# Starting bytes of weight buffers and operands moved by 64 in a two-block transformer kernel

## The chip, the core and the metric

The kernel runs as one launch on one core of a Trainium2 chip. The metric is the device time of that launch in microseconds (us), the median of the runs. Matrix products run on TensorE (PE); its weight loads are listed apart (PEld), since they run beside its matmuls. VectorE (DVE), ScalarE (ACT) and GpSimd (POOL) do the rest, and SyncE (SP) issues the weight transfers.

## What is computed

Two blocks, one after the other, on 256 tokens of width 1024. The first block also carries 256 context tokens. In its first layer all 512 tokens need an output; in its last layer (`l = 1`) the context is only read, so most products there move 256 tokens. The second block moves 256 tokens throughout.

```python
def first_block(...):            # DEPTH = 2
    for l in range(DEPTH):
        x, xc = trunk_layer(...)     # rmsnorm, w_in, latent attention + pooling + gated linear
                                     # attention, merge of the three branches, w_out, rmsnorm
def second_block(...):           # DEPTH = 2
    for layer in range(DEPTH):
        h = rmsnorm_2(x, norm_mix_pre[layer])
        m = attention_mixer(h, ...) if layer % 2 == 0 else recurrent_mixer(h, ...)
        x = x + rmsnorm_2(m, norm_mix_post[layer])
        h = rmsnorm_2(x, norm_ffn_pre[layer])
        x = x + rmsnorm_2(swiglu(h, ...), norm_ffn_post[layer])
def swiglu(h, w_gate, w_up, w_down):             # hidden width 2816
    return (jax.nn.silu(h @ w_gate) * (h @ w_up)) @ w_down
```

## The kernel before

**The weight stream.** All large weights come as 384 "halves" of 128 x 1024 fp32 words (`STREAM`, indexed by k). SP sends half k to a slot of SBUF (`RAW`), ACT rounds it to its high part (`WH`, line 1280), DVE forms the low part (`WL`, line 1874, in the place of the raw words), and TensorE multiplies. A slot is 8 KB in each partition: `WL` in the first 4 KB, `WH` in the last 4. `slots()` gives each half the least recently used slot of those that `free_slots(k)` allows; the order of the halves is fixed.

**One column.** A product of fp32 accuracy is three passes: high weights by high activations, high by low, low by high. `column(k, ...)` (its matmuls are recorded at line 651, in the helper `product`) does this over eight 128-row tiles, so one half is 24 matmuls, each with 128 columns of weights held and 256 tokens moved past them. I call such a group of 24 a column. `some_columns` (line 669) does three columns at once, tile by tile, behind a norm; `pre_normed` (lines 1054 and 1056) does the fourth, with one plain fp32 product of ones by `PB_` in its middle. The down projection has its matmuls at line 1083, its last three halves at line 1094, and `last_column` (line 730) ends the other projections. In `token_rows` (line 1066) the activations are held and the weights move.

**Places.** SBUF places are written by hand as byte offsets from `base`, which lies on a multiple of 128. Slots 0 to 3 stand at 0, 8, 16 and 24 KB. Everything after the held constants stands at `kb(n)`, which is `o + n * 1024`; the sizes of the held tensors make `o` 56384, that is 64 modulo 128. So slots 0 to 3 start at 0 modulo 128, and every other slot and every moving operand (`XH`, `XL`, `XH2`, `XL2`, `YH`, `YL`, `HH`, `HL`, `AH`, `AL`, `CH`, `CL`) at 64 modulo 128. Steps inside a slot or an operand are multiples of 128 bytes. Where 256 tokens move, a column whose weights stand in slots 0 to 3 thus **differs** modulo 128 from what moves past it; a column in any other slot is **alike** to it.

**Which slot when.** From the second block on the slots go round in a cycle of nine: 10, 11, 12, 8, 2, 9, 3, 0, 1, so five columns of nine are alike. The 40 columns of line 651 in the first feed-forward are 21 alike and 19 different, in the second 23 and 17; the 19 columns of line 1083 are 12 and 7 in the first, 10 and 9 in the second. From `merge, 1` to `rg_out` other slots (17, 27 to 33) take part as well. In the order of TensorE's rows below, the number behind the underscore is only the number of the allocation.

Of the kernel before, what the change touches and what calls it, by code (L numbers as in the profile page):

```python
# [9 lines left out]
KT = D // P  # L10
SEQ, CTX = 256, 256
# [14 lines left out]


HALF = 8 * P
PLAN = {}


def plan():
    at = 0
    for l in range(DEPTH):
        for name, n in (("mod", 12), ("win", 12), ("gv", 2), ("merge", 18), ("wout", 4)):
            PLAN[name, l] = at
            at += n
    for name, n in (("attn_qk", 8), ("attn_v", 4), ("attn_out", 4), ("gate_up0", 22), ("down0", 11),
                    ("rg_in", 8), ("rg_ai", 2), ("rg_out", 4), ("gate_up1", 22), ("down1", 11)):
        PLAN[name] = at  # L40
        at += n
# [63 lines left out]
def mod_halves(p):  # L105
# [3 lines left out]
    at = [4 * quarter + rows_ for quarter in ((s, s + 2) if p < MOD_START else (2 * s, 2 * s + 1))]  # L109
    return [2 * PLAN["mod", 0] + a if a < 24 else 2 * PLAN["mod", 1] + a - 24 for a in at]  # L110

# [18 lines left out]
def stream():  # L130
# [13 lines left out]
    for l in range(DEPTH):  # L144
        win = PLAN["win", l]
        for b in FIRST:
# [3 lines left out]
        for place in steps_of(l):  # L150
            for kind, i in place:
# [4 lines left out]
                elif kind == "gv":  # L156
                    group(("gv", l, i), PLAN["gv", l], 2 * i, 2)
                else:
                    mod_pair(i)
        group(("merge", l), PLAN["merge", l], 0, 36)  # L160
        group(("wout", l), PLAN["wout", l], 0, 8)
# [23 lines left out]
STREAM, AT = stream()  # L185
# [29 lines left out]
LATE = BLOCK2 + 5  # L215

HIDDEN, DOWN_LATE = 5, AT["down0"] + 9
NSLOT = 34
END, MORE = 28, 5


def free_slots(k):

    if k < MOD_START:
        return [0, 1, 2, 3, 5, 13, 14, 15, 16]
    if k < AT["z", 0, FIRST[0]]:
        return [0, 1, 2, 3, 5, 14, 16]
    if k < AT["g", 0, 0]:
        return [4, 6, 7, 17]
    if k in WHOLE and k < AT["merge", 0]:  # L230
        return [25, 26]
    if k < AT["merge", 0] + END:
        return [0, 1, 2, 3]
    if k < AT["wout", 0] + 8:
        return [0, 1, 2, 3, 7, 17]
    if k < AT["z", 1, FIRST[0]]:
        return [18, 19, 20, 21, 22, 23, 24, 25]
    if k < AT["g", 1, 0]:
        return [0, 1, 2, 3, 7, 8, 17]
    if k < AT["merge", 1] + MORE:  # L240
        return [0, 1, 2, 3, 8]
    if k < AT["merge", 1] + END + 3:
        return [0, 1, 2, 3, 8, 27, 28]
    if k < BLOCK2:
        return [0, 1, 2, 3, 8, 10, 17, 27, 28]
    more = [29, 30, 31] if AT["rg_x"] <= k < AT["rg_a0"] else [32, 33] if DOWN_LATE <= k < AT["rg_x"] else []
    return [0, 1, 2, 3, 8, 9, 10] + ([11, 12] if k >= LATE else []) + more

OPENED = ((7, AT["merge", 0] + END, AT["merge", 0] + 25), (17, AT["merge", 0] + END, AT["merge", 0] + 25),
          (25, AT["g", 0, 0], AT["g", 0, 0]), (26, AT["g", 0, 0], AT["g", 0, 0]),
          *((s, AT["wout", 0] + 8, AT["wout", 0] + 1) for s in range(18, 26)), (8, AT["z", 1, FIRST[0]], AT["wout", 0] + 3),
          (27, AT["merge", 1] + MORE, AT["merge", 1] + 1), (28, AT["merge", 1] + MORE, AT["merge", 1] + 1),
          (10, AT["merge", 1] + END + 3, AT["merge", 1] + 25), (17, AT["merge", 1] + END + 3, AT["merge", 1] + 25),
          (29, AT["rg_x"], AT["down0"] + HIDDEN), (30, AT["rg_x"], AT["down0"] + HIDDEN), (31, AT["rg_x"], AT["attn_out"] + 8),
          (32, DOWN_LATE, AT["down0"]), (33, DOWN_LATE, AT["down0"]),
          (9, BLOCK2, AT["wout", 1] + 3), (11, LATE, AT["wout", 1] + 8), (12, LATE, AT["wout", 1] + 8))


def slots():

    slot, nth, before, last, uses = [], [], [], {}, {}
    for k in range(HALVES):
        s = min(free_slots(k), key=lambda s: last.get(s, -1))
        uses[s] = uses.get(s, 0) + 1
        slot.append(s)
        nth.append(uses[s])
        before.append(max([last.get(s, -1) + 1] + [count for s_, first, count in OPENED if s_ == s and k >= first]))
        last[s] = k  # L270
    return slot, nth, before

# [30 lines left out]
def program(nc, x_t, wstream, small, vecs, consts, rel, consts2, out_t):  # L303
    f32 = mybir.dt.float32
    f32r = mybir.dt.float32r
# [4 lines left out]
    LN_EXP, EXP_TANH = "natural_log_exp_and_others", "exp_and_others"  # L310

    with ExitStack() as ctx:
        base = (nc.sbuf_base + 63) // 64 * 64
        KB_ = 1024

        def sb(name, at, *shape, dt=f32):
            return nc.alloc_sbuf_tensor_at(name, [P, *shape], dt, offset=base + int(at))
# [6 lines left out]
        at = 48 * KB_  # L324
# [8 lines left out]
        MOD, AMOD, GPOST = held("MOD", DEPTH * 3 * KT, 2), held("AMOD", DEPTH * KT, 2), held("GPOST", DEPTH * KT, 2)  # L333
        NLAM, PLAM, LT = held("NLAM", KT), held("PLAM", KT), held("LT", 2, KT)
        STAT, SELT, R2C = held("STAT", 2, 8), held("SELT", 4), held("R2C", 2)
        o = at

        def kb(n):
            return o + n * KB_

        SLOT_AT = [8 * KB_ * i for i in range(4)] + [kb(113), kb(121), kb(133), kb(141), kb(48), kb(134), kb(142), kb(16), kb(24),
                                                   kb(0), kb(8), kb(16), kb(24), kb(80),
                                                   *(kb(103 + 4 * i) for i in range(7)), kb(134), kb(138),
                                                   kb(109), kb(125), kb(62), kb(70), kb(126), kb(0), kb(8)]
        RAW = [sb(f"RAW{i}", a, HALF) for i, a in enumerate(SLOT_AT)]
        WL = [sb(f"WL{i}", a, HALF, dt=f32r) for i, a in enumerate(SLOT_AT)]
        WH = [sb(f"WH{i}", a + 4 * KB_, HALF, dt=f32r) for i, a in enumerate(SLOT_AT)]

# [10 lines left out]
        WIDE = [TOK, SEQ]  # L361
        ZG = [sb(f"ZG{l}", kb(32), 12, w) for l, w in enumerate(WIDE)]
        YL = [sb(f"YL{l}", kb(32), 12, w, dt=f32r) for l, w in enumerate(WIDE)]
        YH = [sb(f"YH{l}", kb(133), 4, w, dt=f32r) for l, w in enumerate(WIDE)]
        Z = sb("Z", kb(56), 12, TOK)
        VG = sb("VG", kb(80), 4, 512)
        SW = sb("SW", kb(88), SW_MORE + NSW)
# [4 lines left out]
        CS = sb("CS", kb(150), SEQ + 2 * PADW)  # L372
        DF = sb("DF", kb(151) + 64, SEQ)
        MG = [sb(f"MG{l}", kb(101), KT, w) for l, w in enumerate(WIDE)]
        SG = [sb(f"SG{l}", kb(117), KT, w) for l, w in enumerate(WIDE)]
        EX, EM = sb("EX", kb(88), 4, TOK), sb("EM", kb(96), TOK)
        E1 = sb("E1", kb(56), TOK)
        QE, KDT = sb("QE", kb(68), TOK), sb("KDT", kb(70), NCH, P)
# [3 lines left out]
        LG = Z[:, Z_POOL:Z_POOL + 4, :]  # L382


        M = sb("M", kb(32), KT, SEQ)
        SQ2 = sb("SQ2", kb(40), KT, SEQ)
        PA = sb("PA", kb(56), 2, SEQ)
        PB_ = sb("PB", kb(58), SEQ)
        R1, R2, R2Q = sb("R1", kb(59), SEQ), sb("R2", kb(60), SEQ), sb("R2Q", kb(61), SEQ)
        aS, aA = kb(62), kb(78)  # L390
        XH2 = sb("XH2", kb(0), KT, SEQ, dt=f32r)
        XL2 = sb("XL2", kb(8), KT, SEQ, dt=f32r)

# [71 lines left out]

        raw_in = [sem(f"raw_in{i}") for i in range(NSLOT)]
        hi_ready, lo_ready, halves_done = sem("hi_ready"), sem("lo_ready"), sem("halves_done")
# [94 lines left out]
        def _(pool):  # L562
# [17 lines left out]
            def post_sum(blocks):  # L580
                sum_blocks(msq_ready, SQ2, PA, PB_, blocks, lambda b: b)
                n.next(msq_ready, KT)
# [48 lines left out]
        def _(pe):  # L631
# [102 lines left out]
            def first_block(l):  # L734
                t, w = query_tokens(l), WIDE[l]
                ring = (0, 1) if l == 0 else (0, 1, 2)
                zg, yh, yl = ZG[l], YH[l], YL[l]

# [286 lines left out]
                for kt in some_columns(k0, outs3, xh, xl, range(KT)):  # L1025
                    pe.wait_ge(xl_ready, n.next(xl_ready))
                pb, sq = (PB0, SQ) if l == 0 else (PB_, SQ2)
                for i in range(3, 7):
# [40 lines left out]
            def ffn(i):  # L1069
# [18 lines left out]
                for m in range(KT):  # L1088
                    if m == KT - 1:
                        sums = take(4)  # L1090
                        post_sum_part(sums, SEQ, PB_, SQ2, 4)
                    for u in range(FB - TAIL, FB):
# [4 lines left out]
                    if m < KT - 1:  # L1097
                        last.then_inc(down_ready, 1)
                post_sum_end(sums, SEQ, SQ2)

            def attention():
# [109 lines left out]
                for i in range(3, 7):  # L1211
                    column(k0 + i, take((0, 1, 2, 6, 7)[i % 5])[:, 0:SEQ], lambda kt: AH[:, kt, :], lambda kt: AL[:, kt, :])
                last_column(k0 + 7, take(2)[:, 0:SEQ], lambda kt: AH[:, kt, :], lambda kt: AL[:, kt, :], SEQ, PB_, SQ2)

# [45 lines left out]
        def _(act):  # L1260
# [57 lines left out]
            def first_block(l):  # L1318
                t, w = query_tokens(l), WIDE[l]
                zg, yh, sg, mg = ZG[l], YH[l], SG[l], MG[l]  # L1320
                lead = (4 if l == 0 else 5) - 2
# [217 lines left out]
            def normed_block(m, b, gain):  # L1539

                A(SQ2[:, m, :], BANK[b][:, 0:SEQ], ACT.Square).then_inc(msq_ready, 1)
                A(M[:, m, :], BANK[b][:, 0:SEQ], ACT.Copy, scale=gain(m)).then_inc(bank_free[b], 1)

# [310 lines left out]
        def _(dve):  # L1854
# [93 lines left out]
            def first_block(l):  # L1948
                t, w = query_tokens(l), WIDE[l]
                zg, yh, yl, sg, mg = ZG[l], YH[l], YL[l], SG[l], MG[l]  # L1950
                lead = (4 if l == 0 else 5) - 2
# [346 lines left out]
            def boundary(gain):  # L2298
# [5 lines left out]
                def scaled(c):  # L2304
                    k0, k1 = CHUNKS[c]
                    v.tensor_tensor(M[:, k0:k1, :], M[:, k0:k1, :], R1[:, :].unsqueeze(1).to_broadcast([P, k1 - k0, SEQ]),
                                    ALU.mult).then_inc(mr_step, 1)
                    n.next(mr_step)

                def added(c):  # L2310
                    k0, k1 = CHUNKS[c]
                    dve.wait_ge(mr_step, m0 + c + 1)
                    v.tensor_tensor(X[:, k0:k1, XT], X[:, k0:k1, XT], M[:, k0:k1, :], ALU.add).then_inc(x_new, 1)

# [406 lines left out]
```

## Time and profile before

| what | value |
|---|---|
| median of 3 runs | 1565.04 us (1564.38 to 1567.49) |
| the profiled execution: device time | 1563.12 us |
| its span, first to last instruction | 1561.3 us |
| TensorE busy, matmuls | 1457.5 us, 93% |
| VectorE, ScalarE busy | 897.9 us (58%), 723.2 us (46%) |
| chain of work that ended last: TensorE's share | 81% |
| mean granted TensorE clock | 0.972 |

A matmul of 256 columns is recorded with a duration of about 280 ns, but matmuls overlap in the array: what a stretch costs is the distance from the start of one to the start of the next. A start is given to 0.01 us, so the distance is best read over the 24 matmuls of a column. The mean durations by group of instructions don't tell it.

### The profile page before, as it was taken

What the parts mean: (1) busy time and instruction counts of PE and PEld (TensorE: products, weight loads), DVE (VectorE), ACT (ScalarE), POOL (GpSimd) and SP (SyncE); (2) the same over time, 40 slices, a digit from 0 to 9 for tenths busy, and PEclk for the clock granted to TensorE, in tenths of its full rate; (3) what the DMA queues carried; (4) which work ended last, traced back from release to release, by engine and by line L of the source; (5) the groups of instructions that cost most, each with busy time, mean ns of one, the idle gap of its engine ahead of it and who ended that gap; (6) DMA issues with size and microseconds to landing.
All of it is one profiled execution on the core that took longest, in us unless ns stands there. A gap on an engine that the chain in (4) does not pass through costs nothing.

```text
span 1561.3 us, 23755 instructions
## 1 busy us (share of the span) xinstructions
PE 1457.5 (93%) x9888; PEld 1263.1 (81%) x9888; DVE 897.9 (58%) x1495; ACT 723.2 (46%) x1164; POOL 98.8 (6%) x125
## 2 busy tenths in 40 slices
PE   4999999999999998999999899989999988899997
PEld 2676766787877776777988799878999988899997
DVE  4455663535443625776376558766666567766642
ACT  4433333523325244544545545665444468644442
POOL 0200000000000030000000010001221000112200
PEclk8999999899999999999999999999999999899998
DMA  8433333122223271232344455424656625356661
GB/s 341 128 108 123 121 122 115 50 80 80 82 71 113 73 259 43 93 95 68 107 150 135 150 189 195 135 92 152 189 189 210 229 76 176 109 182 189 186 189 52
DMA packets 58841, 212.56 MB, mean 136 GB/s; under 512 B 6448, under 2 KB 7728, under 8 KB 58736
## 3 DMA queue, kind: packets, MB, share of 16 engines
q1 hardware_dynamic: 57408, 205.29, 40.3%
q0 software_dynamic: 1328, 5.77, 1.2%
q8 instruction: 79, 1.29, 0.3%
q14 instruction: 26, 0.21, 0.0%
HBM read 209.98 MB, written 1.05 MB: 135 GB/s over the span
## 4 chain that ended last, share of the span: by engine, by line
PE 81%; DVE 10%; ACT 5%; DMA 1%; issue 1%; SPq 0%; POOL 0%; ACTq 0%; DVEq 0%; POOLq 0%
PE B L651 51%; PE B L669 8%; PE B L1083 7%; DVE WL L1874 3%; PE B L795 3%; ACT WH L1280 2%; PE B L1066 1%; DMA RAW<-wstream 1%; PE B L1094 1%; PE B L681 1%; PE B L875 1%; PE B L862 1%; PE B L989 1%; PE B L730 1%; PE B L1056 1%
## 5 line engine op out<-in xcount | busy, mean ns | idle before, releaser
L1874 DVE TENSOR_TENSOR WL<-RAW,WH 128x1024 fp32r<-128x1024 f32 x336 | 412.4, 1235 | 384.5 <-ACT WH L1280 383.0
L651 PE MATMUL B<-XH,WH 128*128 128x256 f32 (+1 forms) x1600 | 510.9, 319 | 4.3 <-DVE ZG L2085 2.7
L651 PE MATMUL B<-XL,WH 128*128 128x256 f32 (+1 forms) x1600 | 495.2, 309 | 0.0
L651 PE MATMUL B<-XH,WL 128*128 128x256 f32 (+1 forms) x1600 | 495.1, 309 | 0.0
L1280 ACT ACTIVATE WH<-RAW 128x1024 fp32r<-128x1024 f32 x336 | 346.4, 1052 | 112.3 <-DMA RAW<-wstream 112.0
L651 PEld LDWEIGHTS B<-XH,WH 128*128 128x128 f32 x1600 | 305.1, 191 | 31.7 <-issue 7.9
L651 PEld LDWEIGHTS B<-XL,WH 128*128 128x128 f32 x1600 | 305.2, 191 | 21.3 <-issue 5.9
L651 PEld LDWEIGHTS B<-XH,WL 128*128 128x128 f32 x1600 | 305.0, 191 | 17.0
L669 PE MATMUL B<-XH,WH 128*128 128x256 f32 (+1 forms) x208 | 73.4, 353 | 25.3 <-DVE XL L2318 13.3
L1083 PE MATMUL B<-HH,WL 128*128 128x256 f32 x304 | 85.3, 280 | 0.0
L1083 PE MATMUL B<-HH,WH 128*128 128x256 f32 x304 | 85.2, 280 | 0.0
L1083 PE MATMUL B<-HL,WH 128*128 128x256 f32 x304 | 85.2, 280 | 0.0
L1586 ACT ACTIVATE SIL<-T 128x256 f32<-128x256 f32 x44 | 18.4, 418 | 121.0 <-DVE T L2335 121.0
L651 PE MATMUL B<-YH,WH 128*128 128x512 f32 (+1 forms) x192 | 66.0, 344 | 8.3 <-DVE ST L2202 6.6
L669 PEld LDWEIGHTS B<-XH,WH 128*128 128x128 f32 x208 | 44.4, 214 | 34.5 <-issue 24.4
L669 PE MATMUL B<-XL,WH 128*128 128x256 f32 (+1 forms) x208 | 71.8, 345 | 0.0
L669 PE MATMUL B<-XH,WL 128*128 128x256 f32 (+1 forms) x208 | 71.5, 344 | 0.0
L1387 ACT ACTIVATE PR<-B,STAT 128x512 f32<-128x512 f32 (+1 forms) x48 | 29.6, 616 | 87.6 <-DVE STAT L2075 87.6
L1502 ACT ACTIVATE SG<-B 128x512 f32<-128x512 f32 (+1 forms) x48 | 23.5, 490 | 97.1 <-PE B L651 97.1
L651 PE MATMUL B<-YL,WH 128*128 128x512 f32 (+1 forms) x192 | 64.7, 337 | 0.0
L651 PE MATMUL B<-YH,WL 128*128 128x512 f32 (+1 forms) x192 | 64.6, 337 | 0.0
L575 POOL TENSOR_TENSOR PA<-SQ 128x512 f32<-128x512 f32 (+1 forms) x6 | 11.6, 1938 | 805.4 <-ACT SQ L1521 482.9
(326 smaller groups left out, 2444.6 us busy)
## 6 DMA issues: line engine op xcount, KB each, us to landing
RAW<-wstream SPq DMA_DIRECT2D x384, 512.0 KB, 3.5
X<-x_t SPq DMA_DIRECT2D x4, 512.0 KB, 6.6
SW<-small POOLq DMA_DIRECT2D x2, 896.0 KB, 8.5
SW<-small POOLq DMA_DIRECT2D x2, 768.0 KB, 7.3
BT<-rel POOLq DMA_DIRECT2D x1, 1024.0 KB, 15.1
X<-consts POOLq DMA_DIRECT2D x1, 768.0 KB, 8.6
out_t<-X SPq DMA_DIRECT2D x3, 256.0 KB, 2.4
BT<-rel POOLq DMA_DIRECT2D x1, 512.0 KB, 10.8
```

Of the source, the lines that this page charges most:

```text
L651: last = mm(out, w, x, start=i == 0, stop=i == len(pairs) - 1)
L669: last = mm(out, w[:, kt * P:(kt + 1) * P], x(kt, h), start=i == 0 and p == 0, stop=i == KT - 1 and p == 2)
L681: last = mm(bank[at:at + 32, :], cv[:, 2 * (p % 4) + j, :], raw_of(k + c)[:, j * 512:(j + 1) * 512], start=p % 4 == 0, stop=p % 4 == 3, ti ...
L730: last = mm(out, wt[:, kt * P:(kt + 1) * P], x(kt), start=kt == 0 and p == 0, stop=kt == KT - 1 and p == 2)
L795: last = mm(bank, x[:, kt, rows_], wt[:, cols], start=kt == 0 and p == 0 and tb % 2 == 0, stop=kt == KT - 1 and p == 2, skip_group_check=True)
L862: last = nc.tensor.transpose(bank[:, k * P:(k + 1) * P], PR[:, u % 2, k * P:(k + 1) * P], ident)
L1083: last = mm(outs[m][:, 0:SEQ], w[:, m * P:(m + 1) * P], h[:, u, :], start=u == 0 and p == 0, stop=False)
L1280: A(hi_of(h), raw_of(h), ACT.Copy).then_inc(hi_ready, 1)
L1387: A(PR[:, u % 2, 0:nk], BANK[b][:, 0:nk], ACT.Exp, bias=STAT[:, u % 2, 0:1], accum_out=STAT[:, u % 2, 1:2]).then_inc(bank_free[b], 1)
L1502: A(sg[:, i, :], bank_of("G", l, b, i)[:, 0:w], ACT.Tanh, scale=0.5).then_inc(free("G", l, b, i), 1)
L1586: A(SIL[:, f % 2, :], T1[:, f % 2, :], ACT.Silu).then_inc(silu_ready, 1)
L1874: v.tensor_tensor(lo_of(h), raw_of(h), hi_of(h).bitcast(f32), ALU.subtract).then_inc(lo_ready, 1)
```

## The change

`base` is rounded to 128 instead of 64 (it comes to the same byte), and `o` is written so that it is 64 modulo 128 (it comes to the same byte as well). The slots used where 256 tokens move are shifted by 64 bytes (9, 10 and 31 by 192) and so start at 0 modulo 128: 9 to 12 and 27 to 33. Slot 8, which also serves the last layer of the first block, keeps its place; from `wout, 1` on a new slot 34, the same place plus 64 bytes, takes its turns, and `OVER` makes it wait for slot 8's last reader. Slots 0 to 7 and 13 to 26 keep their places; of these slot 17 has a turn in `merge, 1` and in `wout, 1`. Around the shifted slots the tensors of the second block make room: `M`, `SQ2`, `PA`, `PB_`, `R1`, `R2`, `R2Q` and everything at `aS` move by 64 bytes, everything at `aA` (`HH`, `HL`, `AH`, `AL`, `CH`, `CL` among them) by 128, `YH` and `SG` of layer 1 by 128 and 64.

No instruction is added or removed, and the order is the same on every engine; which half waits for which (`BEFORE`) is the same too. Only the slot's name changes, as here on TensorE in the first feed-forward, at the step from one column to the next. Before:

```order
L651 MATMUL B6<-XH2_216,WH12_141 128x256
L651 MATMUL B6<-XL2_217,WH12_141 128x256
L651 MATMUL B6<-XH2_216,WL12_107 128x256
L651 MATMUL B7<-XH2_216,WH8_137 128x256
L651 MATMUL B7<-XL2_217,WH8_137 128x256
L651 MATMUL B7<-XH2_216,WL8_103 128x256
```

After:

```order
L665 MATMUL B6<-XH2_219,WH12_143 128x256
L665 MATMUL B6<-XL2_220,WH12_143 128x256
L665 MATMUL B6<-XH2_219,WL12_108 128x256
L665 MATMUL B7<-XH2_219,WH34_165 128x256
L665 MATMUL B7<-XL2_220,WH34_165 128x256
L665 MATMUL B7<-XH2_219,WL34_130 128x256
```

Slot 34 stands where slot 8 stood; nothing else has moved in the row of instructions.

```diff
@@ free_slots(k)
+    if k < AT["wout", 1]:
+        return [0, 1, 2, 3, 8, 10, 17, 27, 28]
     if k < BLOCK2:
-        return [0, 1, 2, 3, 8, 10, 17, 27, 28]
+        return [0, 1, 2, 3, 34, 10, 17, 27, 28]
     more = [29, 30, 31] if AT["rg_x"] <= k < AT["rg_a0"] else [32, 33] if DOWN_LATE <= k < AT["rg_x"] else []
-    return [0, 1, 2, 3, 8, 9, 10] + ([11, 12] if k >= LATE else []) + more
+    return [0, 1, 2, 3, 34, 9, 10] + ([11, 12] if k >= LATE else []) + more
@@ slots()
+OVER = {34: (8,)}
+    def read(s):
+        return max(last.get(other, -1) for other in (s, *OVER.get(s, ())))
@@ program(...)
-        base = (nc.sbuf_base + 63) // 64 * 64
+        base = (nc.sbuf_base + 2 * LINE - 1) // (2 * LINE) * 2 * LINE
-        o = at
+        o = at + (LINE - at) % (2 * LINE)
-        SLOT_AT = [8 * KB_ * i for i in range(4)] + [kb(113), kb(121), kb(133), kb(141), kb(48), kb(134), kb(142), kb(16), kb(24),
-                                                   kb(0), kb(8), kb(16), kb(24), kb(80),
+        SLOT_AT = [8 * KB_ * i for i in range(4)] + [kb(113), kb(121), kb(133), kb(141), kb(48), kb(134) + 3 * LINE, kb(142) + 3 * LINE,
+                                                   kb(16) + LINE, kb(24) + LINE, kb(0), kb(8), kb(16), kb(24), kb(80),
                                                    *(kb(103 + 4 * i) for i in range(7)), kb(134), kb(138),
-                                                   kb(109), kb(125), kb(62), kb(70), kb(126), kb(0), kb(8)]
+                                                   kb(109) + LINE, kb(125) + LINE, kb(62) + LINE, kb(70) + LINE, kb(126) + 3 * LINE,
+                                                   kb(0) + LINE, kb(8) + LINE, kb(48) + LINE]
-        YH = [sb(f"YH{l}", kb(133), 4, w, dt=f32r) for l, w in enumerate(WIDE)]
+        YH = [sb(f"YH{l}", kb(133) + 2 * LINE * l, 4, w, dt=f32r) for l, w in enumerate(WIDE)]
-        PB_ = sb("PB", kb(58), SEQ)
+        PB_ = sb("PB", kb(58) + LINE, SEQ)
-        aS, aA = kb(62), kb(78)
+        aS, aA = kb(62) + LINE, kb(78) + 2 * LINE
```

`LINE` is 64.

## Rows read from the trace of the kernel before

**Rows 1.** The page: chain that ended last, shares by engine.

```profile
PE 81%; DVE 10%; ACT 5%; DMA 1%; issue 1%; SPq 0%; POOL 0%; ACTq 0%; DVEq 0%; POOLq 0%
```

**Rows 2.** Chain in order of time (start, us, what), both feed-forwards.

```profile
1081.36 112.15 PE B L651 x960
1193.51 53.60 PE B L1083 x456
...
1374.78 112.48 PE B L651 x960
1487.26 53.28 PE B L1083 x456
```

**Rows 3.** Timeline of PE (start, duration): columns in slots 1, then 10.

```profile
1114.78 0.28 PE L651 MATMUL B<-XH,WH 128*128 128x256 f32 x1
...
1117.50 0.28 PE L651 MATMUL B<-XH,WH 128*128 128x256 f32 x1
...
1120.38 0.28 PE L651 MATMUL B<-XH,WH 128*128 128x256 f32 x1
```

**Rows 4.** The same view, line 1066, weights moving: end of slot 9, slot 3.

```profile
968.00 0.28 PE L1066 MATMUL B<-WH,XL 128*128 128x256 f32 x1
...
969.08 0.28 PE L1066 MATMUL B<-WH,XL 128*128 128x256 f32 x1
...
970.13 0.28 PE L1066 MATMUL B<-WH,XL 128*128 128x256 f32 x1
...
972.17 0.28 PE L1066 MATMUL B<-WH,XL 128*128 128x256 f32 x1
```

**Rows 5.** The same view: a column in slot 1 behind a plain fp32 product.

```profile
950.15 0.59 PE L1054 MATMUL B<-PB,C 128*128 128x256 f32 x2
950.40 0.47 PE L1056 MATMUL B<-XH,WH 128*128 128x256 f32 x1
950.70 0.28 PE L1056 MATMUL B<-XL,WH 128*128 128x256 f32 x1
...
951.88 0.28 PE L1056 MATMUL B<-XH,WL 128*128 128x256 f32 x1
```

**Rows 6.** The same view, recurrent mixer, slot 3, then 0 and 1.

```profile
1292.21 0.38 PE L651 MATMUL B<-CH,WH 128*128 128x256 f32 x1 [0.87 <-DVE XR L2335]
...
1297.26 0.28 PE L651 MATMUL B<-XH,WH 128*128 128x256 f32 x1
...
1300.09 0.28 PE L651 MATMUL B<-XH,WH 128*128 128x256 f32 x1
```

**Rows 7.** Windows: busy us (instructions) of each engine, PEclk, DMA share, GB/s.

```profile
1080.00:1190.00 110.00, 110.00 (x943) 110.00 (x942) 71.33 (x105) 50.81 (x66) 22.72 (x40) 1.00 0.62 195
1193.00:1246.00 53.00, 53.00 (x453) 53.00 (x452) 30.92 (x27) 27.18 (x26) 2.00 (x2) 1.00 0.70 236
1274.00:1371.00 97.00, 86.01 (x668) 84.04 (x667) 75.92 (x115) 70.06 (x117) 5.87 (x3) 0.93 0.43 136
```

**Rows 8.** Chain in order of time: the second block's attention, then the recurrent mixer.

```profile
952.16 11.51 PE B L651 x96
...
996.51 3.03 PE B L651 x24
...
1047.91 11.04 PE B L651 x96
...
1319.72 1.24 DVE IG L2530
...
1330.20 11.57 PE B L669 x79
```

More of the change, by code:

```diff
@@ L28 @@
 HALF = 8 * P
+LINE = 64
 PLAN = {}
@@ L217 @@
 HIDDEN, DOWN_LATE = 5, AT["down0"] + 9
-NSLOT = 34
+NSLOT = 35
 END, MORE = 28, 5
@@ L255 @@
           (10, AT["merge", 1] + END + 3, AT["merge", 1] + 25), (17, AT["merge", 1] + END + 3, AT["merge", 1] + 25),
-          (29, AT["rg_x"], AT["down0"] + HIDDEN), (30, AT["rg_x"], AT["down0"] + HIDDEN), (31, AT["rg_x"], AT["attn_out"] + 8),
+          (34, AT["wout", 1], AT["merge", 1] + 25), (29, AT["rg_x"], AT["down0"] + HIDDEN), (30, AT["rg_x"], AT["down0"] + HIDDEN), (31, AT["rg_x"], AT["attn_out"] + 8),
           (32, DOWN_LATE, AT["down0"]), (33, DOWN_LATE, AT["down0"]),
           (9, BLOCK2, AT["wout", 1] + 3), (11, LATE, AT["wout", 1] + 8), (12, LATE, AT["wout", 1] + 8))
+OVER = {34: (8,)}
 def slots():
     slot, nth, before, last, uses = [], [], [], {}, {}
+    def read(s):
+        return max(last.get(other, -1) for other in (s, *OVER.get(s, ())))
     for k in range(HALVES):
-        s = min(free_slots(k), key=lambda s: last.get(s, -1))
+        s = min(free_slots(k), key=read)
         uses[s] = uses.get(s, 0) + 1
@@ L268, in slots @@
         nth.append(uses[s])
-        before.append(max([last.get(s, -1) + 1] + [count for s_, first, count in OPENED if s_ == s and k >= first]))
+        before.append(max([read(s) + 1] + [count for s_, first, count in OPENED if s_ == s and k >= first]))
         last[s] = k
@@ L374, in program @@
         MG = [sb(f"MG{l}", kb(101), KT, w) for l, w in enumerate(WIDE)]
-        SG = [sb(f"SG{l}", kb(117), KT, w) for l, w in enumerate(WIDE)]
+        SG = [sb(f"SG{l}", kb(117) + LINE * l, KT, w) for l, w in enumerate(WIDE)]
         EX, EM = sb("EX", kb(88), 4, TOK), sb("EM", kb(96), TOK)
@@ L382, in program @@
         LG = Z[:, Z_POOL:Z_POOL + 4, :]
-        M = sb("M", kb(32), KT, SEQ)
-        SQ2 = sb("SQ2", kb(40), KT, SEQ)
-        PA = sb("PA", kb(56), 2, SEQ)
-        PB_ = sb("PB", kb(58), SEQ)
-        R1, R2, R2Q = sb("R1", kb(59), SEQ), sb("R2", kb(60), SEQ), sb("R2Q", kb(61), SEQ)
-        aS, aA = kb(62), kb(78)
+        M = sb("M", kb(32) + LINE, KT, SEQ)
+        SQ2 = sb("SQ2", kb(40) + LINE, KT, SEQ)
+        PA = sb("PA", kb(56) + LINE, 2, SEQ)
+        PB_ = sb("PB", kb(58) + LINE, SEQ)
+        R1, R2, R2Q = sb("R1", kb(59) + LINE, SEQ), sb("R2", kb(60) + LINE, SEQ), sb("R2Q", kb(61) + LINE, SEQ)
+        aS, aA = kb(62) + LINE, kb(78) + 2 * LINE
         XH2 = sb("XH2", kb(0), KT, SEQ, dt=f32r)
```

## The prediction

> **What bounds the kernel now.** I read the chain of work that ended last first: TensorE has 81% of it [rows 1]. The second block shows where: each feed-forward is one unbroken piece, 960 matmuls at line 651 and 456 at line 1083 [rows 2], and the windows over both kinds show TensorE busy all the time, VectorE 71.33 of 110 us at most, the DMA engines at 0.62 to 0.70, the clock at 1.00, which is its 2.4 GHz level [rows 7]. So there the time is matmuls times their distance, and the distance is what to look at next. The timeline gives it over a column of 24. In slot 1, which differs modulo 128 from what moves, a column takes 1117.50 - 1114.78 = 2.72 us, 113.3 ns a matmul. The next, in slot 10, alike, takes 1120.38 - 1117.50 = 2.88 us, 120.0 ns [rows 3]. The instructions, the lengths and the clock are the same.
>
> Does this hold for all? It can be tested on whole pieces. First feed-forward, line 651: 21 alike and 19 different columns, 21 x 2.88 + 19 x 2.72 = 112.16 us; the chain has 112.15. Second: 23 and 17, 112.48; the chain has 112.48. Line 1083: 12 and 7, 53.60; 10 and 9, 53.28; both are as in the chain [rows 2]. So two numbers explain the four pieces. Where the roles are swapped (line 1066, weights move, activations are held) the same pair shows: nine matmuls in 969.08 - 968.00 = 1.08 us, 120.0 ns, in slot 9, and eighteen in 972.17 - 970.13 = 2.04 us, 113.3 ns, in slot 3 [rows 4]. The sign of the difference doesn't matter, then, which bears on the slots moved by 192 and on the operands moved by 128.
>
> **A third distance.** It is the weak point of the change. After a break in TensorE's row, different columns often settle at another distance. Behind the fp32 product by `PB_`, ten matmuls in slot 1 take 951.88 - 950.70 = 1.18 us, 118 ns [rows 5]; after the wait at 1292.21 a whole column in slot 0 or 1 takes 1300.09 - 1297.26 = 2.83 us, 117.9 ns [rows 6]. I call this the slow pace. Of the different columns that I followed behind a break about two thirds take it and a third goes to 113.3. It passes over the step from one different column to the next. In the second block I see it end only in a column that is alike: the next different one is at 113.3 again. The change takes away all alike columns there, and with them what ends the slow pace.
>
> **The change part by part.** (1) *Columns that become different.* Feed-forwards: 24 + 14 + 25 + 11 = 74. At 113.3 each saves 0.16 us: 74 x 0.16 = 11.8 us, all on the chain. Rest of the second block: 35. Behind the norm of the attention 4 x 24 matmuls run unbroken, 11.51 us = 119.9 ns each [rows 8]: the 6 columns of the first projections give 1.0 us. The 7 of the second projections stand singly between softmax steps, and five begin with a break. Here I take the slow pace: a different column with its break is 3.03 us [rows 8], 2.83 and a restart of 0.2, so 0.05 each, with 0.16 for the two of line 1066: 0.6 us. The output projection's 4: 0.5 us. The recurrent mixer's 18 would give 2.9 us, but TensorE is busy only 86.01 of 97 us there [rows 7], the wait in rows 6 is for VectorE's `XR`, and the chain passes through VectorE's `IG` [rows 8]: half, 1.4 us. Last layer of the first block: 13 columns (slots 27, 28, 10, and 34 for 8), between breaks, at 0.05: 0.7 us. Sum: 11.8 + 1.0 + 0.6 + 0.5 + 1.4 + 0.7 = 16.0 us.
>
> (2) *Columns that lose the reset.* Each feed-forward enters behind the `PB_` product, where the slow pace begins (rows 5; I saw it the same way in the other column of this kind whose slot differs). A column at the slow pace instead of 113.3 gives up 0.11 us. The bounds are: none stays slow, 0; all 118 columns of lines 651 and 1083 stay slow, 118 x 2.83 = 333.9 us against 331.5 now [rows 2], so +2.4 us instead of -11.8. The trace doesn't show which: the longest unbroken slow stretch of different columns is some 60 matmuls [rows 6], the longest at 113.3 eight columns at most, but with hundreds of such matmuls and no fall to the slow pace without a break. Whatever ends the slow pace need happen only once in each feed-forward. `PB_` itself moves, too, so that its last pass is now alike to the weight load behind it, which may set either pace. I take the slow pace for about ten columns in all: +1 us.
>
> (3) *Supply.* At 2.72 us a column, VectorE's 71.33 us and ScalarE's 50.81 us for 40 columns [rows 7] stand against 108.8 us of TensorE: they hide. The transfers go from 0.62 to about 0.64 of the DMA engines. Nothing is late next in the feed-forwards. If the cover were gone, TensorE would wait for `WL`, at VectorE's rate, still under 2 us a column. The order and the counts of the slots' waits are unchanged, so slot 34 costs nothing.
>
> (4) *Moved places of the other operands.* No length of VectorE or ScalarE work in the trace depends on the slot's place, so 0; bounds: -1 to +1 us.
>
> The sum is -16.0 + 1 = -15 us. The profiled execution has 1563.12 us (a span of 1561.3 us and 1.8 around it), 1.9 under the median of the runs, so 1565.0 - 15 = 1550 us.
>
> The Trainium skill, page "TensorE: Matmul & The Clock Gate", section "Step-by-step: what each phase is for", speaks against this: TensorE has two independent SBUF read ports, and loading the next weights takes nothing from the running matmul. By that rule places would not matter, and the time would stay 1565. Rows 3 and 4 disagree with the rule, by 6.7 ns a matmul; the rival below on the region carries what is left of it.
>
> **The rivals.**
>
> *Lock: the slow pace holds.* It enters behind `PB_` and nothing ends it. Feed-forwards +2.4 us; elsewhere the alike columns gain 48 x 0.05 = 2.4 us, and some 24 different ones that are at 113.3 now lose 0.11 each, 2.6. Sum about +2.5: 1567. For it: both columns like rows 5, and the steps that the pace survived. Against it: it was never seen for longer than three columns.
>
> *Half: one feed-forward locked, or some ten to fifty columns slow in each.* -4 to -10 us: 1555 to 1561.
>
> *Region, not the remainder.* Slots 0 to 3 are also the only ones in the lowest 32 KB, so the pair in rows 3 could come from where they lie, not from the address modulo 128; the trace can't separate the two. Then a shift by 64 bytes changes nothing: 1565.
>
> *Slower: the lock, at a longer distance.* The places are new (differences of 64 the other way, `PB_` at 0 modulo 128), so the pace that the lock holds need not be 117.9 ns. The 118 columns take 331.5 us now, 117.1 ns on average; from (331.5 + 3.1) / 2832 = 118.2 ns on the kernel is slower than the measurement's bound, and at 120 ns it is 339.8 us, +8.3. Between them I take 118.8: +4.9, 1570. For it: some matmuls in transition take 119 and more. Against it: all settled different columns are at 113.3 or below 118.
>
> **How the numbers follow.** About 0.2%, 3.1 us, is what a measurement of this kernel can tell from no change. Chances: forecast 0.46, half 0.14, lock 0.24, region 0.06, slower 0.10. So faster 0.60; same 0.30, lock and region; slower 0.10. The forecast's own range is 1546 (all 122 columns at 0.16 us: -19.5) to 1554. The range for 8 in 10 leaves out the slower rival and the ends: 1546 to 1568.
>
> **What would show it.** Right: the second feed-forward's two pieces at 40 x 2.72 = 108.8 and 19 x 2.72 = 51.7 us, every column in slots 9 to 12 and 34 at 2.72 us. The lock: both pieces made of 2.83 us, 113.2 and 53.8, in slots 0 to 3 as well, where it is 2.72 now. Region: 2.88 and 2.72 side by side as in rows 3. The sum is wrong if TensorE begins to wait in the feed-forwards, or if the recurrent mixer keeps its length.

## The result, and the profile after

| | before | after |
|---|---|---|
| median, same series of runs | 1564.71 us (1563.98 to 1567.49) | 1553.92 us (1550.68 to 1554.48) |
| ratio, 95% interval | | 0.9931 (0.9911 to 0.9952) |
| profiled execution: device time, span | 1563.12, 1561.3 us | 1554.48, 1552.7 us |

The kernel is faster by 10.8 us. A second series of the changed kernel (`a0_again` below) gave 1552.14 against 1564.15, ratio 0.9929 (0.9911 to 0.9947), 12.0 us. 1550 was forecast.

The page's first lines and its shares of the chain, for [rows 1]: nothing but TensorE's time changed.

```profile
PE 1448.6 (93%) x9888; PEld 1251.4 (81%) x9888; DVE 897.2 (58%) x1495; ACT 723.7 (47%) x1164; POOL 98.9 (6%) x125
...
PE 81%; DVE 10%; ACT 5%; DMA 1%; issue 1%; SPq 0%; POOL 0%; ACTq 0%; DVEq 0%; POOLq 0%
```

The chain in order of time (start, us, what) for [rows 2]. The change adds 14 lines, so L651, L669, L1083 and L1094 of before are L665, L683, L1097 and L1108 here.

```profile
1081.76 109.35 PE B L665 x960
1191.11 52.11 PE B L1097 x456
...
1370.81 108.80 PE B L665 x960
1479.61 52.43 PE B L1097 x456
```

Both feed-forwards are still one unbroken piece, and the second one's first part is 108.80 us: 40 columns at 2.72 us and not one at another distance. The other three are a little above 108.8 and 51.7. The timeline of TensorE (start, duration) shows the reason, for [rows 3]. These are the first matmuls of five columns in a row, in slots 1, 10, 11, 12 and 34:

```profile
1090.08 0.28 PE L665 MATMUL B<-XH,WH 128*128 128x256 f32 x1
...
1092.90 0.28 PE L665 MATMUL B<-XH,WH 128*128 128x256 f32 x1
...
1095.73 0.28 PE L665 MATMUL B<-XH,WH 128*128 128x256 f32 x1
...
1098.46 0.28 PE L665 MATMUL B<-XH,WH 128*128 128x256 f32 x1
...
1101.18 0.28 PE L665 MATMUL B<-XH,WH 128*128 128x256 f32 x1
```

The columns in slots 1 and 10 take 2.82 and 2.83 us, those in slots 11 and 12 take 2.73 and 2.72. So the slow pace, there from the column behind the norm as rows 5 had it, passes over five columns of this line and ends in slot 11, with no alike column near. In the four pieces 5, 4, 0 and 7 columns are slow, 16 in all.

The windows (columns as in [rows 7]) for the first feed-forward's two parts and the recurrent mixer:

```profile
1080.00:1190.00 110.00, 110.00 (x966) 109.97 (x965) 71.82 (x106) 51.96 (x68) 23.99 (x42) 1.00 0.63 201
1192.00:1243.00 51.00, 51.00 (x449) 51.00 (x448) 30.19 (x26) 26.00 (x25) 2.00 (x2) 1.00 0.71 244
1270.00:1367.00 97.00, 85.41 (x666) 83.39 (x665) 75.83 (x114) 70.06 (x117) 5.86 (x3) 0.91 0.41 136
```

**Where the time went.** The chain rows of before and after divide the span at the same instructions:

| stretch | before | after | difference | forecast |
|---|---|---|---|---|
| up to the first feed-forward's piece | 1081.36 | 1081.76 | +0.4 | -3.3 |
| its two parts | 165.75 | 161.46 | -4.3 | -5.3 |
| from there to the second one's piece | 127.67 | 127.59 | -0.1 | -2.0 |
| its two parts | 165.76 | 161.23 | -4.5 | -5.3 |
| the rest | 20.76 | 20.66 | -0.1 | -0.2 |
| span | 1561.3 | 1552.7 | -8.6 | -16.0, and +1 for slow columns |

The first line hides something that isn't the change's. In the first layer, whose slots and order are untouched, after has 3.3 us more. TensorE alone over the same instructions (columns: TensorE busy, PEclk, DMA share, GB/s), first before, then after:

```profile
437.00:500.00 63.00, 59.15 (x275) 1.00 0.28 92
```

```profile
437.00:503.30 66.30, 62.45 (x273) 0.95 0.27 87
```

The granted clock was 1.00, the 2.4 GHz level, before, and 0.95 on average after; it fell to its 1.2 GHz level for two stretches of 3.4 us, and 0.05 x 66.3 = 3.3 us. Without that the first line would be -2.9, and the whole -12.0 us. These two are estimates for one place, not measurements: over the whole execution the granted clock was 0.972 before and after, so what the changed kernel lost here it was spared elsewhere. In the recurrent mixer it was 0.93 before ([rows 7]) and 0.91 after. The gain is therefore best read from the pieces at a clock of 1.00, which have -4.3 and -4.5 us.

### The profile page after: what moved, and what is told of

Its sections match the earlier page's. It is cut to its first block, busy times and chain, and to the rows that moved or that the text cites. A ratio compares the mean times of both kernels' runs of the same rounds, so it can differ in the third digit from the quotient of the medians.

```text
span 1552.7 us, 23755 instructions
## 1 busy us (share of the span) xinstructions
PE 1448.6 (93%) x9888; PEld 1251.4 (81%) x9888; DVE 897.2 (58%) x1495; ACT 723.7 (47%) x1164; POOL 98.9 (6%) x125
## 4 chain that ended last, share of the span: by engine, by line
PE 81%; DVE 10%; ACT 5%; DMA 1%; issue 1%; SPq 0%; POOL 0%; ACTq 0%; DVEq 0%; POOLq 0%
PE B L665 51%; PE B L683 8%; PE B L1097 7%; DVE WL L1888 3%; PE B L809 3%; ACT WH L1294 2%; PE B L1080 1%; DMA RAW<-wstream 1%; PE B L1108 1%; PE B L695 1%; PE B L889 1%; PE B L876 1%; PE B L1003 1%; PE B L744 1%; PE B L1070 1%
## 5 line engine op out<-in xcount | busy, mean ns | idle before, releaser
L665 PE MATMUL B<-XH,WH 128*128 128x256 f32 (+1 forms) x1600 | 507.6, 317 | 4.3 <-DVE ZG L2099 2.7
L665 PE MATMUL B<-XL,WH 128*128 128x256 f32 (+1 forms) x1600 | 491.5, 307 | 0.0
L665 PE MATMUL B<-XH,WL 128*128 128x256 f32 (+1 forms) x1600 | 491.4, 307 | 0.0
L1294 ACT ACTIVATE WH<-RAW 128x1024 fp32r<-128x1024 f32 x336 | 346.7, 1053 | 108.8 <-DMA RAW<-wstream 108.5
L665 PEld LDWEIGHTS B<-XH,WH 128*128 128x128 f32 x1600 | 303.0, 189 | 32.2 <-issue 8.2
L665 PEld LDWEIGHTS B<-XL,WH 128*128 128x128 f32 x1600 | 303.1, 189 | 21.7 <-issue 6.1
L665 PEld LDWEIGHTS B<-XH,WL 128*128 128x128 f32 x1600 | 302.9, 189 | 17.0
L683 PE MATMUL B<-XH,WH 128*128 128x256 f32 (+1 forms) x208 | 73.1, 352 | 25.3 <-DVE XL L2332 13.3
L1097 PE MATMUL B<-HH,WH 128*128 128x256 f32 x304 | 84.3, 277 | 0.0
L1097 PE MATMUL B<-HH,WL 128*128 128x256 f32 x304 | 84.3, 277 | 0.0
L1097 PE MATMUL B<-HL,WH 128*128 128x256 f32 x304 | 84.2, 277 | 0.0
L665 PE MATMUL B<-YH,WH 128*128 128x512 f32 (+1 forms) x192 | 66.8, 348 | 8.3 <-DVE ST L2216 6.4
L683 PEld LDWEIGHTS B<-XH,WH 128*128 128x128 f32 x208 | 44.0, 212 | 34.7 <-issue 24.4
L683 PE MATMUL B<-XL,WH 128*128 128x256 f32 (+1 forms) x208 | 71.3, 343 | 0.0
L683 PE MATMUL B<-XH,WL 128*128 128x256 f32 (+1 forms) x208 | 71.1, 342 | 0.0
L665 PE MATMUL B<-YL,WH 128*128 128x512 f32 (+1 forms) x192 | 65.4, 340 | 0.0
L665 PE MATMUL B<-YH,WL 128*128 128x512 f32 (+1 forms) x192 | 65.1, 339 | 0.0
## 6 DMA issues: line engine op xcount, KB each, us to landing
BT<-rel POOLq DMA_DIRECT2D x1, 512.0 KB, 10.6
```

Of the source, the lines that this page charges most:

```text
L665: last = mm(out, w, x, start=i == 0, stop=i == len(pairs) - 1)
L683: last = mm(out, w[:, kt * P:(kt + 1) * P], x(kt, h), start=i == 0 and p == 0, stop=i == KT - 1 and p == 2)
L1097: last = mm(outs[m][:, 0:SEQ], w[:, m * P:(m + 1) * P], h[:, u, :], start=u == 0 and p == 0, stop=False)
L1294: A(hi_of(h), raw_of(h), ACT.Copy).then_inc(hi_ready, 1)
```

## The experiments

Each edit is against the changed kernel. Places are told from `base`, modulo 256. In the changed kernel slots 0 to 3, 9, 10 and 31 stand at 0, slots 11, 12, 27 to 30, 32, 33 and 34 at 128; `XH2` and `XL2` stand at 64, `HH`, `HL`, `AH`, `AL`, `CH` and `CL` at 192. I call a column **minus** when its weights stand 64 below what moves, and **plus** when 64 above. With `XH2` slots 0 to 3, 9 and 10 are minus and the others plus; with `HH` it is the reverse. In `token_rows`, where the weights move, I take the sign of what is held against what moves.

The theory: the difference of the two places modulo 128 decides. The rivals: the region of SBUF; a period of 256; any difference will do. Then, since 16 columns stayed slow: what sets the slow pace, and what ends it.

**Shift by 128 instead of 64** (`e1_by128`, one execution).

```diff
-        ... kb(134) + 3 * LINE, kb(142) + 3 * LINE, kb(16) + LINE, kb(24) + LINE, ...
+        ... kb(134) + 256, kb(142) + 256, kb(16) + 128, kb(24) + 128, ...
-        aS, aA = kb(62) + LINE, kb(78) + 2 * LINE
+        aS, aA = kb(62) + 128, kb(78) + 128
```

The other places that the change shifts by 64 are shifted by 128 too.

> The shifted slots are moved by 128 bytes (9, 10 and 31 by 256) instead of 64, so that they are alike to what moves modulo 128 again, but differ modulo 256; everything else is laid out as in the changed kernel. Theory (the remainder modulo 128 decides): columns in slots 9 to 12 and 34 take 2.88 us again, the feed-forward pieces about 112.2, 53.6, 112.5 and 53.3 us, total about 1564. Rival (a longer period, 256 or more, or any difference of places helps): 2.72 us, total about 1554.

```profile
1085.31 112.15 PE B L665 x960
1197.46 54.20 PE B L1097 x456
```

1568.80 us; one execution of before beside this and the next three runs had 1566.30. The first part is back at 112.15, to the last digit what [rows 2] has. A period of 256 falls: those columns are nowhere near 113.3 ns. That the sum is the same is chance, though: per matmul slots 9 and 10 take 120 ns with `XH2`, slots 11, 12 and 34, whose places are 128 off, mostly 118.5 to 118.9, and slot 2 behind them 117.7, where it had 113.3 before. Slots 3, 0 and 1 are at 113.3 with `XH2` but for their first turn in the second feed-forward, and with `HH` slots 0 to 3 are at 118 but for three columns. So 256 does play a part, in which distance beside 113.3 a column gets.

**The lowest slots made alike** (`e2_low_alike`, one execution). Slots 0 to 3, `X` and the held constants move up by 64; what stands behind them keeps its remainder.

```diff
-        SLOT_AT = [8 * KB_ * i for i in range(4)] + ...
+        SLOT_AT = [64 + 8 * KB_ * i for i in range(4)] + ...
```

> The changed kernel with slots 0 to 3 moved by 64 bytes, so that these four are now the ones alike to what moves, while slots 9 to 12 and 34 stay different. Theory (remainder): columns in slots 0 to 3 take 2.88 us wherever 256 tokens move, the others 2.72 or 2.83; the 40 columns of line 665 in the first feed-forward about 19 x 2.88 + 21 x 2.72 = 111.8 us. Where 512 tokens move, the columns in slots 0 to 3 come to 227 ns a matmul from about 231, some 5 us in all. Total about 1560. Rival (the lowest 32 KB of SBUF are a region of their own): slots 0 to 3 stay at 2.72 us, total 1554.

```profile
1084.23 111.84 PE B L665 x960
...
1374.92 111.74 PE B L665 x960
```

1562.19 us. The first is the 111.8 us expected. The roles have changed over: with `XH2` 120 ns in slots 0 to 3, 113.3 in slots 9 to 12 and 34, but for two columns at 117.8 at the start of the second. The region falls; it is the remainder.

**Shift by 32, and by 96** (`e3_by32`, `e4_by96`, one execution each).

```diff
-        ... kb(16) + LINE, kb(24) + LINE, ...
+        ... kb(16) + 32, kb(24) + 32, ...
```

> The shifted slots are moved by 32 bytes (9, 10 and 31 by 160) instead of 64: weights start 32 above what moves, modulo 128. Theory (two streams collide when they are in the same 64 bytes of a 128-byte line): 32 is half a collision, so a distance between 113.3 and 120.0 ns in slots 9 to 12 and 34, total 1556 to 1562. Rival A (any difference will do): 113.3 ns, total about 1554. Rival B (only exactly 64 helps): 120.0 ns, total about 1564.

> The shifted slots are moved by 96 bytes (9, 10 and 31 by 224): weights start 96 above, that is 32 below what moves, modulo 128. Theory (same 64 bytes): as with 32, a distance between 113.3 and 120.0 ns, total 1556 to 1562. Rival A (what counts is which stream is ahead): the two signs of 32 give different distances, one of them 113.3. Rival B (only exactly 64): 120.0 ns, total about 1564.

By 32, then by 96:

```profile
1078.54 113.65 PE B L665 x960
...
1372.41 111.92 PE B L665 x960
```

```profile
1081.96 113.31 PE B L665 x960
```

1561.04 and 1564.17 us. In the pieces shown first the moved slots take 118 to 120 ns with 32 and 117 to 119 with 96, and slots 0 to 3, whose own difference is still 64, are at 118 as well. So "any difference" falls too: among those tried only 64 gives 113.3 for a whole feed-forward. Nor are these 64's slow pace, brought in from the neighbours. In the second piece with 32, slots 0 to 3 are at 113.3 to 113.8 and the moved slots between them still at 118.2 to 119.7; at line 1097 with 96, slots 0 to 3 are at 113.3 to 114.2, slots 11, 12 and 34 at 116.7 to 116.8 and slots 9 and 10 mostly at 120.1. So 32 and 96 have distances of their own, mostly nearer to 120.0 than to 113.3.

**The changed kernel again** (`a0_again`, 6 executions).

> The changed kernel once more, beside the kernels that follow. Every theory: about 1554 us, ratio 0.993. Theory on the slow pace (it ends at a step from weights 64 below to weights 64 above what moves, modulo 256, and at no other step between different columns): the same columns as in its first profile are slow, those in slots 9, 3, 0, 1, 10 behind the product by PB_ in the first feed-forward, and if line 1097 starts slow, up to the step from slot 34 to slot 2. Rival (it ends by chance): other columns.

1552.14 us (1550.83 to 1556.51). The slow columns of its first feed-forward are the same nine, 109.35 and 52.11 us; in the second there are eight at line 665, where the first profile had none, and the same seven at line 1097. In the feed-forwards of both executions every slow stretch at line 665 ends from slot 10 to slot 11, every one at line 1097 from slot 34 to slot 2. With `XH2` and with `HH`, both are steps from a minus column to a plus one. That gave the next theory: the sign matters, and that step is what ends the slow pace.

**All columns plus** (`e5_plus`, 12 executions, and `e5_again`, 8).

```diff
-        SLOT_AT = [8 * KB_ * i for i in range(4)] + [..., kb(134) + 3 * LINE, kb(142) + 3 * LINE,
+        SLOT_AT = [128 + 8 * KB_ * i for i in range(4)] + [..., kb(134) + 320, kb(142) + 320,
-        aS, aA = kb(62) + LINE, kb(78) + 2 * LINE
+        aS, aA = kb(62) + 64, kb(78) + 256
```

> All slots used where 256 tokens move stand 64 bytes above what moves, modulo 256 (slots 0 to 3 and all behind them moved by 128, slots 9, 10 and 31 by 320 instead of 192, the operands of the second block and YH by 256). Slots 8 and 17 stay alike in the last layer of the first block. Theory (sign modulo 256): behind a break the slow pace ends within some five matmuls, no feed-forward column stays slow, pieces of lines 665 and 1097 at 108.8, 51.7, 108.8 and 51.7 us, total 1 to 4 us under the changed kernel, 1550 to 1553. Rival (chance): some columns stay slow as now, total 1554.

> The kernel of e5_plus once more, for a trace of one of its long executions: its profiled one took 1552.65 us, while most others took 1568 to 1571. Theory (with one sign the pace drawn behind the break holds): in an execution of 1568 us or more both feed-forwards are slow from end to end, pieces 113.1 and 53.7 us, as in e6_minus, 17 us over the fast one with the other second-block columns; an execution between, near 1560, has one feed-forward slow. Rival (something else is longer, such as waits for weights): pieces at 108.8 and 51.7 us, and the time is lost elsewhere.

The profiled execution of the first series had 1552.65 us:

```profile
1083.22 108.80 PE B L665 x960
1192.02 51.68 PE B L1097 x456
1369.76 108.80 PE B L665 x960
1478.56 51.68 PE B L1097 x456
```

That of the second had 1562.80 us:

```profile
1087.00 108.80 PE B L665 x960
1195.80 51.68 PE B L1097 x456
1373.35 113.07 PE B L665 x960
1486.41 53.71 PE B L1097 x456
```

All 118 columns fast in one; in the other 59 fast, then 59 slow from the first to the last (113.07 / 960 = 117.8 ns). The medians are 1568.84 us, ratio 1.0009 (0.9986 to 1.0032), and 1562.78, ratio 0.9987 (0.9953 to 1.0021): the gain is gone on average, yet single executions of this one kernel go from 1552.65 to 1571.0. The 20 of them lie in three groups: 2 at 1552.7 to 1552.8, 8 at 1559.2 to 1563.9, 10 at 1568.3 to 1571.0. That fits none, one and both feed-forwards slow, and the profiled ones are of the first and second group; one of the third wasn't profiled. Two feed-forwards alone would part the groups by 4.27 + 2.03 = 6.3 us each. Of the 10.2 us between the two profiled executions another 3.8 lie ahead of the first feed-forward, most of it between 860 and 895 us, where the granted clock was 1.00 in one and 0.91 in the other. My expectation, that the slow pace ends within a few matmuls behind a break, falls: it held for 1416 matmuls.

**All columns minus** (`e6_minus`, 12 executions).

```diff
-        ... kb(134) + 3 * LINE, kb(142) + 3 * LINE, kb(16) + LINE, kb(24) + LINE, ...
+        ... kb(134) + 448, kb(142) + 448, kb(16) + 192, kb(24) + 192, ...
```

> All those slots stand 64 bytes below what moves, modulo 256 (the shifts of 64 made 192, slots 9, 10 and 31 by 448, operands and YH by 256). Theory (sign modulo 256): the slow pace that begins behind the product by PB_ never ends inside a feed-forward: up to 40 x 2.83 = 113.1 us at line 665 and 19 x 2.83 = 53.7 at line 1097, both times, so that the gain is gone: 1560 to 1567. Rival (chance): about as the changed kernel, 1553 to 1556.

```profile
1082.23 113.07 PE B L665 x960
1195.30 53.71 PE B L1097 x456
1375.85 113.07 PE B L665 x960
1488.91 53.71 PE B L1097 x456
```

1565.27 us, ratio 1.0000 (0.9985 to 1.0016). Both feed-forwards are slow from end to end, in columns that all differ by 64 modulo 128. So a difference is not enough. Together with `e8_turns` below it says that the gain hangs on both signs being there.

**All plus, and the first layer's weights alike** (`e7_split`, 12 executions). Between `e5_plus` and before there was one more difference, where 512 tokens move: see below. Here the first layer uses slots 35 to 38, the places of slots 0 to 3 but 64 modulo 128, and the rest as `e5_plus`.

```diff
+    low = [35, 36, 37, 38] if k < AT["z", 1, FIRST[0]] else [0, 1, 2, 3]
+    return [low[s] if s < 4 else s for s in chosen_slots(k)]
```

> As e5_plus, and in the first layer, where 512 tokens move, slots 0 to 3 get places of their own that are alike to what moves modulo 128. Theory (the trace of before: 512-column matmuls take 227 ns in alike slots and 229 to 233 in slots 0 to 3): some 1260 matmuls gain about 4.5 ns each where TensorE is on the chain, 4 to 6 us less than e5_plus, 1545 to 1548. Rival (TensorE's wait in the first layer is for others): no more than 2 us.

```profile
1077.09 113.07 PE B L672 x960
...
1370.44 113.07 PE B L672 x960
```

1558.72 us, ratio 0.9952 (0.9929 to 0.9975), single executions from 1545.35 to 1564.51; 1545 to 1548 was expected. The profiled one was slow in both feed-forwards. Against `e5_plus` the first layer saves 1378 x 5.5 ns = 7.6 us (below), most of the 10.1 between the medians, and the spread stays.

**Minus and plus in turn** (`e8_turns`, 5 executions). Slots 0 to 3 back to minus, all others plus, with `XH2` and `HH` at one remainder, so that each cycle of nine has two steps from minus to plus (slot 2 to 9 and slot 1 to 10) and no change of sign from the operand.

```diff
-        ... kb(134) + 3 * LINE, kb(142) + 3 * LINE, kb(16) + LINE, ...
+        ... kb(134) + 320, kb(142) + 320, kb(16) + 64, ...
-        aS, aA = kb(62) + LINE, kb(78) + 2 * LINE
+        aS, aA = kb(62) + 64, kb(78) + 256
```

> As e5_plus, but slots 0 to 3 keep their old places: they stand 64 bytes below what moves, modulo 256, all other slots 64 above; the operands all have one remainder. So the sign turns from minus to plus twice in the cycle of nine slots, 2 to 9 and 1 to 10. Theory (a step from weights below to weights above ends the slow pace, and with one sign alone whatever pace was drawn at the break holds): no feed-forward column is slow beyond the first such step, pieces about 108.8, 51.8, 109.1 and 51.8 us; total 1 to 2 us under the changed kernel, 1550 to 1552, and runs within 5 us of each other. Rival (e5_plus was slow for another reason, its shifted held tensors or slots 9, 10 at 320): the median is near that of e5_plus, 1565 or more.

```profile
1078.58 108.82 PE B L665 x960
1187.40 51.68 PE B L1097 x456
1364.68 108.80 PE B L665 x960
1473.48 51.68 PE B L1097 x456
```

1548.97 us (1547.58 to 1551.88), ratio 0.9903 (0.9886 to 0.9920), on a chip where before had 1565.11. Its places differ from those of `e5_plus`, modulo 256, in slots 0 to 3, `X` and the held constants alone, and its median is 13.8 us under that of `e5_again` and 19.9 under that of `e5_plus`. Some 4.8 us of either are the first layer's, where slots 0 to 3 are minus again (see below); the rest goes with the pace.

**Both together** (`e9_split_turns`, 6 executions), and **the changed kernel with the first layer's weights alike** (`e10_split_after`, 5 executions). The first is `e8_turns`, the second the changed kernel, each with slots 35 to 38 for the first layer. In both the cycle of nine also has slot 2 ahead of slot 34 instead of behind it.

> As e8_turns, with places of their own for slots 0 to 3 in the first layer, alike modulo 128 to what moves there (64 bytes further on). Theory: 1380 matmuls of 512 columns go from 229.8 to 227.8 ns, 2.8 us less than e8_turns: 1547 to 1549. Rival (TensorE waits for others in the first layer, so the gain is lost): as e8_turns.

> The changed kernel with that one addition, places of their own for slots 0 to 3 in the first layer. Theory: 2.8 us less than the changed kernel, about 1549 to 1550, 512-column matmuls at 227.8 ns in all slots; the 256-column ones as in the changed kernel, some 16 feed-forward columns slow. Rival: no change, 1552.

`e9_split_turns`:

```profile
1073.08 109.23 PE B L672 x960
1182.31 51.68 PE B L1104 x456
1359.25 109.02 PE B L672 x960
1468.26 51.68 PE B L1104 x456
```

1544.56 us (1542.21 to 1550.71), ratio 0.9879 (0.9858 to 0.9900): the fastest of all, 20.6 us under before on the same chip. It is 4.4 us under `e8_turns`, where 2.8 were expected, and the rest can be the clock's luck: between the two profiled executions 2.85 us have come by 456 us, in the first layer, and another 3.3 come around 858 to 898 us of `e8_turns`, where the granted clock was 0.91 against 1.00. The medians of the granted clock over the executions are 0.977 and 0.974. `e10_split_after` has 1550.27 us (1546.14 to 1551.17), ratio 0.9908 (0.9890 to 0.9925). In the first feed-forward of `e9_split_turns` four columns are slow, in slots 9, 3, 0 and 1; the next, in slot 10, is fast: its first step from minus to plus.

**What ends the slow pace, counted.** I followed each column of the second block where the weights are held and 256 tokens move, in ten profiled executions (before, the changed kernel twice, and `e5_plus` to `e10_split_after` with `e5_again`), into the next where nothing waits between. Of the steps that a slow column makes to another that differs:

| step | fast from there on | still slow |
|---|---|---|
| minus to plus | 31 | 4 |
| plus to minus | 0 | 19 |
| plus to plus | 0 | 263 |
| minus to minus | 0 | 206 |

In the other direction, a fast column passes to a slow one only where the moving operand changes as well, to one whose place isn't the same modulo 256 (`XH2` to `HH`, `CH` to `XH2`): 8 steps, all in the three executions of kernels with operands at 64 and at 192. In the kernels with one remainder for all operands there is none. In `token_rows` of `e8_turns`, which isn't in the table, there is one, from slot 2 (113.3 ns) to slot 9 (117.8): there the weights are what moves, and the two slots differ modulo 256.

**Where 512 tokens move.** `X` and `YH` of the first layer stand at 64. Chain rows of two columns in a row in low slots, for before, `e9_split_turns` and `e5_plus`:

```profile
324.10 11.20 PE B L651 x48
```

```profile
323.14 11.12 PE B L672 x48
```

```profile
326.72 11.40 PE B L665 x48
```

Each row takes in the whole record of its last matmul, 0.39 us, so that before has (11.20 - 0.39) / 47 = 230 ns. Over all unwaited matmuls of this kind in these slots the mean distance is 229.8 ns when minus (before), 227.8 ns when alike (`e9_split_turns`) and 233.3 ns when plus (`e5_plus`). There are some 1378. So plus costs 1378 x 3.5 ns = 4.8 us in `e5_plus`, and alike is worth 1378 x 2.0 ns = 2.8 us in `e9_split_turns`. At 512 tokens alike is the best of the three, at 256 the worst.

## Why the prediction was right, and where its sizes were off

**The step that carried it held.** Two distances, told apart by the place modulo 128, explained the four pieces of before, and 40 x 2.72 = 108.8 us was met to the last digit. Region is refuted by `e2_low_alike`. The rule of the Trainium skill, page "TensorE: Matmul & The Clock Gate", section "Step-by-step: what each phase is for", that loading the next weights takes nothing from the running matmul, would have left 1565 us. The runs differ from it, by 6.7 ns a matmul between alike places and places 64 apart; that it is the load that slows the matmul is a reading, no run here takes the load away.

**Slow columns.** Ten were taken, at +1 us; 16 came in the pieces, at 2.827 - 2.72 = 0.107 us each 1.7 us. The 66 alike columns at 0.16 are 10.6, less 1.7 makes 8.9; the pieces went from 331.51 to 322.69, that is 8.8. This term is closed.

**Everything else that was to gain.** From the end of the first feed-forward's pieces to the second one's, 2.0 us were forecast and 0.1 came. Most of that was the recurrent mixer's 1.4, the half share. TensorE's waits there (what for, us in total, times, longest us), over 1255 to 1371 us of before, then 1250 to 1367 us of after:

```profile
PE B L669 <- DVE CL L2547: 4.4, 1, 4.4
...
PE B L651 <- DVE XR L2335: 0.9, 1, 0.9
```

```profile
PE B L683 <- DVE CL L2561: 4.8, 1, 4.8
...
PE B L665 <- DVE XR L2349: 1.0, 1, 1.0
```

TensorE was busy for 0.6 us less (86.01 and 85.41 of 97 us, [rows 7] and above) and waited 0.5 us longer for VectorE: part of the gain turned into waiting. The rest was never made: the moved column in slot 10 and two of those with `CH`, in slots 11 and 12, run at the slow pace, as slots 0 and 1 did already (rows 6). The half share was the term that was mis-sized: 1.4 us forecast, about nothing measured, and `a0_again` has 127.32 us for the stretch of 127.67 and 127.59. That waiting for VectorE forces it to nothing isn't shown: `e8_turns`, with nine slow columns in the mixer, takes 125.60 us for the same stretch, a part of it by 3.4 us less at the low clock. Up to the first feed-forward the forecast was 3.3 and the gain, without the clock's 3.3 us, 2.9.

**The lock rival** was given 0.24. Its mechanism is real: the slow pace passes from column to column without end, 113.07 and 53.71 us against its 113.2 and 53.8, in `e6_minus` and `e7_split`. That it doesn't decide here comes from a step of the prediction that was wrong, "The sign of the difference doesn't matter". It was read off rows 3 and 4, which both show settled fast columns of one sign each. The change happens to mix the signs: slots moved by 64 are plus, those moved by 192 minus. That is luck: the prediction had no reason to want both. Had it moved slots 9 and 10 by 320, slots 0 to 3 by 128 and the operands by 256, with the same differences modulo 128, it would have been `e5_plus`, and on average no faster than before. The range's upper end, 1568, was there for this case, and the medians of the one-signed kernels `e5_plus`, `e5_again` and `e6_minus`, 1562.78 to 1568.84, lie about there.

**The slower rival** needed a distance above 118.2 ns in locked columns. They are at 117.8.

**Open.** Why the step from minus to plus ends the slow pace, and what sets the pace behind a break, isn't shown: `e5_plus` and `e5_again` are the same kernel with other draws. The four steps from minus to plus that stayed slow aren't explained; all four are in the recurrent mixer. Nor was it tried to alternate column by column.

## What to carry to other kernels

Read TensorE's cost as the distance from start to start, apart for each weight buffer, before believing that equal instructions cost the same. Where 256 fp32 tokens move past 128 columns of weights, put weights and operand 64 bytes apart modulo 128, let buffers with weights 64 below be followed by buffers 64 above, and keep all moving operands at one remainder modulo 256; where 512 move, put them alike. A kernel whose columns all have one sign must be timed many times over, since one execution may show 1552.65 us and the next 1568.96. All this rests on one kernel; and on moving operands of 256 and 512 tokens alone.

## What the runs showed of the hardware

- One kind of matmul (128 x 256, fp32, at the 2.4 GHz level) has three settled distances here: 120.0 ns (alike), 113.3 ns and 117.8 ns (64 apart modulo 128). Where the places are alike modulo 128 but 128 apart modulo 256, it is mostly 118.5 (`e1_by128`).
- The last two are two paces of the same places. The pace outlives 59 columns, 1416 matmuls, and from column to column, among columns that differ, it changes with no wait only at a step in sign or in operand. It differs between executions of one kernel: by 6.3 us in the feed-forwards of the two profiled ones of `e5_plus`, and by an estimated 118 x 0.107 = 12.6 us where both feed-forwards change.
- A difference of 32 or 96 bytes gives 116.5 to 120.2 ns, nowhere near 64's 113.3.
- For 512 tokens the order turns round: 227.8 ns alike, 229.8 ns with the weights 64 below, 233.3 ns with them 64 above.
